# Hybrid SGU and sparse-attention block: order of output steps, late selection steps, weight blocks, norms and key turns changed

## The reference, cut to what matters

```python
h = rmsnorm(x, norm_gain[l])
proj = jnp.einsum('bsd,de->bse', h, w_in[l])
a_u, a_v, a_z, b_q, b_k, b_v, b_z, i_q, i_k, i_w = split_cols(proj, IN_SIZES)
ya = spatial_gating(a_u, a_v, ...)   # gelu, layernorm, a masked 128x128 mix in each block of 128 rows
# sparse attention, for each block of 128 queries (q and k are normed, one key and value head):
logits = jnp.einsum('bqhd,bsd->bqhs', qib, ki32)
idx_score = jnp.einsum('bqhs,bqh->bqs', jax.nn.relu(logits), wib)
idx_score = jnp.where(admissible[None], idx_score, NEG)     # chunk-causal, chunks of 64
_, sel = lax.top_k(idx_score, topk)                         # 256 keys
scores = jnp.einsum('bqhd,bqkd->bhqk', qb, k_sel) * scale
scores = scores - slopes[None, :, None, None] * dist[:, None]
p = jax.nn.softmax(scores, axis=-1)
yb = jnp.einsum('bhqk,bqkd->bqhd', p, v_sel)
mixed = jnp.concatenate([oa * jax.nn.silu(a_z), ob * jax.nn.silu(b_z)], axis=-1)   # oa, ob: normed ya, yb
x = x + jnp.einsum('bse,ed->bsd', mixed, w_out[l])
```

## Time and profile before

| | us |
|---|---|
| median of 3 runs | 565.14 (564.82 to 565.28) |
| profiled execution | 565.3 |
| its span | 563.5 |
| PE busy | 545.6 |
| DVE busy | 444.0 |
| ACT busy | 371.5 |

### The profile page before, as it was taken

How to read it: one execution, slowest core, us unless ns; L and a number is a source line. 1 busy time by engine, 2 the same in 40 slices (tenths; PEclk the granted TensorE clock), 3 DMA queues, 4 the chain that set the end, 5 groups by cost and what they waited for, 6 DMA issues and landing times. The chain is left out here.

```text
span 563.5 us, 8936 instructions
## 1 busy us (share of the span) xinstructions
PE 545.6 (97%) x2974; PEld 461.4 (82%) x2974; DVE 444.0 (79%) x1107; ACT 371.5 (66%) x711; POOL 180.0 (32%) x283
## 2 busy tenths in 40 slices
PE   8999999999999999999999999989999999999997
PEld 8997788878888888887888887768788789889886
DVE  4775777899889998999878888887878787866631
ACT  5885667767997767777988566756465555755510
POOL 1760000014449997667210003551112021202130
PEclk9999999999999999999999999999999999999999
DMA  8623110012331111131212144503030302011032
GB/s 250 214 66 110 57 38 20 1 38 76 112 93 39 38 46 49 39 94 39 56 58 74 52 133 134 170 19 95 19 94 20 94 19 76 20 40 35 1 113 75
DMA packets 39982, 39.69 MB, mean 70 GB/s; under 512 B 6144, under 2 KB 28160, under 8 KB 39936
## 3 DMA queue, kind: packets, MB, share of 16 engines
q1 hardware_dynamic: 38416, 39.11, 22.9%
q10 hardware_dynamic: 1520, 0.01, 0.1%
HBM read 30.72 MB, written 8.39 MB: 69 GB/s over the span
## 5 line engine op out<-in xcount | busy, mean ns | idle before, releaser
L1072 PE MATMUL ps_proj<-w_hi,xT_hi 128*128 128x512 f32 (+1 forms) x432 | 164.7, 381 | 1.2 <-DVE w_lo L1382 1.0
L1072 PE MATMUL ps_proj<-w_lo,xT_hi 128*128 128x512 f32 (+1 forms) x432 | 161.1, 373 | 0.0
L1072 PE MATMUL ps_proj<-w_hi,xT_lo 128*128 128x512 f32 (+1 forms) x432 | 161.1, 373 | 0.0
L912 ACT ACTIVATE ps_lg<-score,cand 128x768 f32<-128x768 f32 (+2 forms) x96 | 96.0, 1000 | 10.4 <-DVE cand L1475 10.4
L1072 PEld LDWEIGHTS ps_proj<-w_lo,xT_hi 128*128 128x128 f32 x432 | 81.4, 188 | 14.8
L1072 PEld LDWEIGHTS ps_proj<-w_hi,xT_hi 128*128 128x128 f32 x432 | 81.4, 189 | 14.5 <-DVE w_lo L1382 2.0
L1072 PEld LDWEIGHTS ps_proj<-w_hi,xT_lo 128*128 128x128 f32 x432 | 81.5, 189 | 11.8
L969 ACT CAST xT_hi<-ps_tp 128x512 fp32r<-128x512 f32 (+3 forms) x96 | 43.0, 483 | 66.0 <-PE ps_tp L1193 66.0
L1696 DVE TENSOR_TENSOR xT_lo<-ps_tp,xT_hi 128x512 fp32r<-128x512 f32 (+3 forms) x96 | 50.4, 553 | 31.4 <-ACT xT_hi L969 31.1
L1382 DVE SCALAR_TENSOR_TENSOR w_lo<-stage,g_in,w_hi 128x512 fp32r<-128x512 f32 x48 | 43.1, 905 | 10.0 <-ACT w_hi L772 9.2
L953 ACT ACTIVATE lo_f<-lo_f,negmax 128x128 f32<-128x128 f32 (+7 forms) x64 | 50.2, 785 | 0.2
(11 more groups left out here) (175 smaller groups left out, 1101.7 us busy)
## 6 DMA issues: line engine op xcount, KB each, us to landing
stage<-in_w_in_dram SPq DMA_DIRECT2D x48, 256.0 KB, 2.7
x_in<-in_x_dram SPq DMA_DIRECT2D x8, 512.0 KB, 6.0
lo_f<-in_x_dram SPq DMA_DIRECT2D x7, 512.0 KB, 4.0
out_dram<-lo_f SPq DMA_DIRECT2D x7, 512.0 KB, 3.5
q_scratch<-nat SPq DMA_DIRECT2D x8, 256.0 KB, 2.1
q_in<-q_scratch SPq DMA_DIRECT2D x8, 256.0 KB, 3.6
stage<-in_w_out_dram SPq DMA_DIRECT2D x8, 256.0 KB, 2.7
z_scratch<-nat SPq DMA_DIRECT2D x8, 256.0 KB, 2.1
```

The costliest lines, as they stand in the source:

```text
L912: act.activation(ps_lg[i % 2][:, 0:keys(t)], score[:, sc_off[t]:sc_off[t] + keys(t)], ACT.Sign, bias=cand[:, t:t + 1].bitcast(F32), scale= ...
L1072: mm = pe.matmul(ps_proj[u % 2][:, 0:n], a[:, k, rows], b[:, k, 0:n], start=(k == 0 and i == 0), stop=(k == KB - 1 and i == 2))
```

## The change

Seven edits. The IQ weights lag one block instead of two, and the keys of tile 6 are turned (`kT(6)`), and copied (`hi_k`, `lo_k`), behind the last of these weight blocks. `qiT(t+1)` comes before block 1 instead of block 2 (from the third IQ tile on). The first search step and `q_norm(0)` stand behind the head sums of tile 7 instead of ahead of them. From m=16 on the output steps are 1, 3, 2, 3, 2, 2, 2, 1 by head instead of 2 each. `add_res(t-2,0)` stands at h=3 instead of h=4 behind `lo_q`. The last weight blocks are made a head earlier for the most part. The late selection steps stand at h = 2, 4 in tile 1, and from tile 4 on at h = 1, 3, 5, 7 instead of 0, 2, 4, 6.

```diff
--- before.py
+++ after.py
@@ -89,7 +89,7 @@
 
     WARM_0, WARM_1 = 14, 20
     ROUNDS_FROM = 2
-    IQ_W_BEHIND = 2
+    IQ_W_BEHIND = 1
     SPLIT = 5
     sc_off = {t: sum(keys(s) for s in range(T0, t)) for t in range(T0, T)}
     SC_COLS = sum(keys(t) for t in range(T0, T))
@@ -384,7 +384,7 @@
                 if n % KB == KB - 1:
                     last_units[m] = FREE + n // KB
         FIRST_HALF_W_AT = {2: FREE, 5: FREE + 1, 9: FREE + 2, 12: FREE + 3}
-        W_AT = (16, 16, 17, 17, 20, 21, 22, 23)
+        W_AT = (15, 15, 16, 17, 19, 20, 21, 22)
         BY_POOL = 4
 
         def pv_bank(n):
@@ -814,12 +814,13 @@
                 if t + 2 < T:
                     hi_x(t + 2)
                     square_x(t + 2)
-                if t > 0:
+                if 0 < t < T - 1:
                     hi_k(t - 1)
                 if t >= IQ_W_BEHIND:
                     hi_w(KB + t - IQ_W_BEHIND)
             for k in range(KB - IQ_W_BEHIND, KB):
                 hi_w(KB + k)
+            hi_k(T - 2)
 
             nat_free = {
 
@@ -1116,7 +1117,7 @@
                 def between(k):
                     if T0 <= t:
                         logit(t, k)
-                    if k == 2 and t + 1 < T:
+                    if k == (2 if t <= T0 else 1) and t + 1 < T:
                         qiT(t + 1)
                 return between
 
@@ -1134,11 +1135,16 @@
                 project(KVI, t)
                 if t + 2 < T:
                     xT(t + 2)
-                if t > 0:
+                if 0 < t < T - 1:
                     kT(t - 1)
+
+            def late_keys(k):
+                if k == 2:
+                    kT(T - 2)
+
             for t in range(T0, T):
                 if t == T0:
-                    project(IQ, t)
+                    project(IQ, t, late_keys)
                 else:
                     project(IQ, t, index(t - 2))
                 if t == T0:
@@ -1272,13 +1278,13 @@
             pe.wait_ge(act_counted, (T - SPLIT) * 32)
             scores(0, 0)
             scores(0, 1)
-            STEPS = 2
-            assert STEPS * H == 2 * KB
+            STEPS = {1: 3, 2: 2, 3: 3, 4: 2, 5: 2, 6: 2, 7: 1, 0: 1}
+            assert sum(STEPS.values()) == 2 * KB
             pending = last_projections()
             for t in range(T):
                 for h in range(H):
                     m = head_no(t, h)
-                    steps = STEPS_BZ[m] if m < len(STEPS_BZ) else STEPS
+                    steps = STEPS_BZ[m] if m < len(STEPS_BZ) else STEPS[h]
                     for i in range(steps):
                         if i == steps - 1:
                             if h == Q_AT and t + 1 < T:
@@ -1297,7 +1303,7 @@
                     pT(t, h)
                     if m + 2 < T * H:
                         scores(*divmod(m + 2, H))
-            for _ in range(STEPS):
+            for _ in range(STEPS[0]):
                 next(pending)
             mT(T - 2, 0)
             mT(T - 2, 1)
@@ -1393,12 +1399,13 @@
                 if t + 2 < T:
                     lo_x(t + 2)
                 k_norm(t)
-                if t > 0:
+                if 0 < t < T - 1:
                     lo_k(t - 1)
                 if t >= IQ_W_BEHIND:
                     lo_w(KB + t - IQ_W_BEHIND)
             for k in range(KB - IQ_W_BEHIND, KB):
                 lo_w(KB + k)
+            lo_k(T - 2)
 
             def lo_qi(t):
                 for odd in range(2):
@@ -1616,9 +1623,14 @@
                 if t == 1:
                     sum_heads(T - 1, KB * AV + 1)
                     dve.memset(delta[:, T - 1:T], 0).then_inc(cand_ready, 1)
+                if t == 1:
+                    background(True, False)
+                    q_norm(0)
                 if t >= 2:
                     lo_w(KB * AV + t)
                 q_sums(t)
+                if t == 0:
+                    continue
                 background(True, False)
                 q_norm(t)
                 background(False, t >= ROUNDS_FROM)
@@ -1658,7 +1670,7 @@
 
             late = late_steps()
 
-            LATE_AT = ((2, 4, 6), (2, 4, 6), (0, 2, 4, 6))
+            LATE_AT = ((2, 4, 6), (2, 4), (0, 2, 4, 6), (0, 2, 4, 6), (1, 3, 5, 7))
 
 
             def twice_silu(t):
@@ -1753,10 +1765,10 @@
                     if h == MIX_AT and t > 1:
                         lo_mix(t - 2, 0)
                         lo_mix(t - 2, 1)
+                    if h == 3 and t > 1:
+                        add_res(t - 2, 0)
                     if h == Q_AT and t + 1 < T:
                         lo_q(t + 1)
-                    if h == 4 and t > 1:
-                        add_res(t - 2, 0)
                     if m + 2 < T * H:
                         if t < 4:
                             bias_max(*divmod(m + 2, H))
@@ -1775,7 +1787,7 @@
                         lo_w(KB * O2 + W_AT.index(m))
                     if m < 2:
                         lo_w(KB * O1 + TANH_FROM - 1 + m)
-                    if h in LATE_AT[min(t, 2)]:
+                    if h in LATE_AT[min(t, 4)]:
                         next(late, None)
             add_res(T - 3, 1)
             lo_mix(T - 2, 0)
```

## The result

The changed kernel takes 572.88 us (572.07 to 575.14) against 565.21 (564.82 to 565.34), six runs each: ratio 1.0145, interval 1.0122 to 1.0168. It is slower, as forecast, but by 7.7 us where 3.3 were forecast, and outside the range. The profiled execution is the dearest of its runs: 575.14 us, span 573.3 against 563.5.

The account below looks back on a forecast made before the run. PE's work was taken to set the time, so its stalls were added up: -3.45 - 0.3 - 0.6 + 7.8 = +3.45 on the profiled 565.3 us gives 568.7, as a median 568.5. The range was 561.8 to 570.5.

Parts of the forecast that it names:

- The three edits upstream: Ahead of the attention: index weights and tile 6 keys, qiT, first search step with q_norm(0); gain 3.45 us, taken in full.
- qiT: Index stage: qiT one block earlier removes small PE stalls on the relu; gain 0.9 us, bounds 0.5 and 1.2.
- q_norm(0): First search step and q_norm(0) behind tile 7's head sums: PE's gap at 117.65 goes; gain 1.3 us (1.1 to 1.4).
- The cover for q_norm(0): Third to fifth q tile: the later q_norm(0) and its store stay hidden from PE, with 3 us to spare.
- Tiles 4 to 7: Attention: fewer output steps at tile starts and moved late steps make PE wait for transpose slots; 7.8 us lost.
- Tiles 2 and 3: Attention: weight blocks and add_res net a 0.3 us gain, and the wait at 396.01 gives 0.6 more.
- The clock: PE's clock might drop behind stalls of over 2 us at m=32 and m=44; one case in a hundred.
- The reading on headroom: Weight loads' busy share read as room would let PE absorb stalls and shrink losses; left out because start spacing stays constant.
- the 82%: The busy share of PE's weight loads in the profile before; not counted as room to absorb stalls.
- (a): Faster: slots do not bind as counted, losses of tiles 4 to 7 only 1.5 us; 562.3 us, chance 0.25.
- (b): About equal: each of the three tile starts costs 0.8 us less than counted; 564.7 us, chance 0.14.
- (c): Slower still: the search stage swallows the upstream gain; 572 us if whole, 570.2 if half; chance 0.09.

Follow-up runs that it names:

- experiment 5: The changed kernel with dummy identity transposes keeping PE busy in its waits; 570.63 us, ratio 1.0091.
- up: The changed kernel with all attention edits undone, keeping only the three edits ahead of the attention; 561.11 us, ratio 0.9923.
- experiment 2: up plus the changed kernel's output steps 1,3,2,3,2,2,2,1 and add_res at h=3; 571.22 us, ratio 1.0093.
- experiment 7: The changed kernel with the late selection steps where they were before; 566.21 us, ratio 1.0019.
- experiment 4: up plus the changed kernel's weight block placement (W_AT); 560.86 us, ratio 0.9920.
- experiment 6: The changed kernel with two output steps for each head and add_res behind lo_q at h=4, as before; 565.55 us, ratio 1.0008.
- experiment 9: The kernel before with only qiT(t+1) moved before block 1 instead of block 2; 563.79 us.
- experiment 1: The run of up: the three edits ahead of the attention alone, the attention as in the kernel before; 561.11 us, ratio 0.9923.
- experiment 11: up with the scan of 1024 keys moved from behind m=40 to m=42, between the sums of y and lo_pT; 559.78 us, ratio 0.9898.

## Why the prediction was wrong

With the clock held (experiment 5) the exps of the heads stand, against the kernel before, at -4.50 for head 0, -2.89 for head 32 and +5.08 for head 63, and the span at +5.1. The forecast's sum to compare with is +3.45. The 5.1 are -4.5 upstream, +1.6 in tiles 2 and 3 and +8.0 behind them.

- **The three edits upstream** (-3.45 forecast, -4.3 measured alone in sum). The mechanism was right in all three. Two sizes were off: qiT, -1.5 instead of -0.9, and q_norm(0), -1.5 instead of -1.3. The cover for q_norm(0) held.
- **Tiles 4 to 7** (+7.8 forecast, -2.89 to +5.08 = +8.0 measured). Tile by tile, from the exp of one tile's first head to that of the next and for tile 7 to the end of the span, against up: 3.0 (forecast 2.9), 2.3 (2.4), 1.9 (1.8), 0.8 (0.7). DVE's timeline of the changed kernel at the start of tile 5, which answers to the earlier trace rows:

```profile
438.40 0.95 DVE L1698 CUSTOM_DVE_ANT_0 lo_f<-ps_lg,score 128x768 f32<-128x768 f32 x1
...
439.28 1.27 DVE L1531 TENSOR_SCALAR_CACHE_REDUCE gt<-score,cand 128x1024 int8<-128x1024 f32 x1
...
440.48 0.69 DVE L1744 TENSOR_TENSOR lo_f<-ps_proj,lo_f 128x512 f32<-128x512 f32 x1
...
441.08 1.28 DVE L1732 TENSOR_TENSOR xT_hi<-ps_tp,mixT_hi 128x512 fp32r<-128x512 f32 x2
```

This is the order that the forecast laid out: row maximum, count of 1024 keys, residual, low parts of mixT, and pT(40) behind it. pT(40) starts 5.62 us after pT(39) (436.29 and 441.91 above); the forecast said 5.7.

- **Tiles 2 and 3** (-0.9 forecast, +1.6 measured with the clock held). This step failed, by 2.5 us, more than any other term of the sum. The forecast took the wait at the first step of the second half to shrink because add_res comes a head sooner, and priced the edits one by one. It put two things at nothing. One is the late edit in tile 1: it moves the scan of 768 keys from head 16 to head 18, directly ahead of add_res(0,0) on DVE, where POOL lengthens it by 1.0. The other is that three steps at h=1 and h=3 outrun the weight blocks (experiment 2), which the weight edit only made good (experiment 7). The kernels separate the edits. The step order brings the first step of the second half forward from h=5 to h=4, yet with the late steps unmoved the wait for add_res(0,0) is 0.20 (experiment 7), as the forecast had it; with them moved it grew from 1.08 to 1.84. From the exp of head 0 to that of head 32 the change against the kernel before is -0.2 with the weight edit (experiment 4), +0.6 with the step order added (7), -0.7 with the late steps added instead (6), +1.6 with all (5). So the step order costs 0.8 where the late steps are unmoved and 2.3 where they are moved: the loss is in the combination. How it divides over the single waits (pT(16) 1.61, add_res(0,0) 1.84, `mT(1,1)` and smaller ones) no run separates; experiment 6 has the first two at 1.62 and 1.92 and loses nothing in this stretch.
- **The clock** (one chance in a hundred, +4.7 in the profiled execution, +2.25 in the median). This is the second failed step. The two together put the time out of range: with the clock held 570.63 is just above the range's upper end, 570.5, and with tiles 2 and 3 as forecast the median would be, by estimate, 572.9 - 2.5 = 570.4. I read the full clock in the earlier trace rows as a property of the kernel, and looked for a fall only behind stalls of over 2 us, at m=32 and m=44. It fell behind 1.61 and 1.84 us as well, at m=16 and m=20. The rule cited there, of the Trainium skill (TensorE: Matmul & The Clock Gate, "Part 1: The HAM clock gate") has the clock at half after idleness, and this trace agrees in kind: PE waits, and behind the wait it runs at the lower level (0.50 from 367 to 370) for a stretch. Whether it falls changes from run to run: behind the wait for weight block 7 it stays full in the trace of the kernel before and falls in that of experiment 9.
- **The reading on headroom.** The Trainium skill (Perfetto Trace Analysis, "Identifying the Most-Contended Engine") judges TensorE's headroom by MFU, the share of its peak arithmetic rate that is used, and by the busy share of weight loads; of matmul busy time it says that it is no good measure, and not, as the prediction has it, that it flatters. The prediction was right to leave the 82% out as room to absorb stalls. This trace shows none absorbed: the -4.22 at head 0 of experiment 1 is -4.16 at head 63, and the waits added in tiles 4 to 7 are there at the end. For this kernel start spacing tells the headroom, and not the weight loads' share.

Of the rivals, (a) and (b) fall by the tile starts, each of which costs what was counted; (c) falls by experiment 1.

## What to carry to other kernels

When PE sets the pace and two slots tie it to VectorE, price a moved VectorE step by what stands right behind it in VectorE's order and how soon PE wants that; where VectorE waited for PE anyway, even the longest step, 2.28 us, was free (experiment 11). Price edits that meet in one stretch together: here the step order cost 0.8 us or 2.3, depending on where a scan stood. Move consumers and producers together: a step order that runs ahead of its weights or of its residual loses more than the stall it was to cover. And add to each stall of PE of the size seen here (1.6 to 2.3 us) the risk of a stretch at half clock, here 1.0 to 1.6 us, which also spreads the run times.

## What the hardware showed that I had not expected

- The changed kernel's runs fall into steps by mean granted clock: 0.997, 0.994, 0.991 at about 572.1, 573.5 and 575.1 us. In one comparison 6 of 21 runs of the kernel before have a lower clock too, and are about 1.0 us longer.
- 90 dummy transposes in PE's waits made the kernel 2.25 us faster and its spread 0.25 us instead of 3.1.
- A scan on VectorE beside a two-input GpSimd instruction takes 2.78 instead of 1.75 us when it starts second, and the other takes 2.72 instead of 1.28 when the scan starts first.
- The last store lands 1.1 us later behind DVE's last residual in the two kernels of experiments 2 and 7 than in the others; why is open.
